# Start of a hybrid-layer kernel: loads queued in order of use, the norm's weight row spread by TensorE, a narrower first projection piece

## The reference

```python
h = jnp.concatenate([meta, x], axis=1)
xn = rms_norm(h, mix_norm_w)                       # the weight row multiplies every token
h = h + hybrid_mixer(xn, w_in, ...)                # proj = xn @ w_in, 3592 columns
h = h + hierarchical_moe(rms_norm(h, ffn_norm_w), ...)   # 32 experts, top 2
out = rms_norm(h, final_norm_w)[:, N_META:]
```

## Time and profile before

| | before |
|---|---|
| median of 3 runs | 1504.84 us (1503.98 to 1507.54) |
| profiled execution | 1506.76 us |
| its span, first to last instruction | 1504.9 us |
| mean granted TensorE clock | 0.935 |
| PE busy | 88% of the span |
| DVE busy | 62% |
| ACT busy | 48% |
| POOL busy | 11% |
| DMA, mean of the span | 182 GB/s |
| chain that ended last, by engine | PE 64%, DVE 13%, ACT 10%, issue 10%, DMA 2% |

### The profile page before, as it was taken

How to read it: one execution, slowest core, us unless ns; L and a number is a source line. 1 busy time by engine, 2 the same in 40 slices (tenths; PEclk the granted TensorE clock), 3 DMA queues, 4 the chain that set the end, 5 groups by cost and what they waited for, 6 DMA issues and landing times.

```text
span 1504.9 us, 20632 instructions
## 1 busy us (share of the span) xinstructions
PE 1318.8 (88%) x7574; PEld 1144.4 (76%) x7574; DVE 932.9 (62%) x1178; ACT 722.3 (48%) x927; POOL 158.7 (11%) x145
## 2 busy tenths in 40 slices
PE   3989998999899989769993389999999999999960
PEld 3979997999799989547772278888888888888840
DVE  4664455445544554332225578888888888888827
ACT  6351234134313430232222067777777777777823
POOL 0010111011102110011110011111111111111000
PEclk9999998999899999659996599999999999999985
DMA  6100010000000000243330379999999999999848
GB/s 194 43 15 29 15 43 16 29 29 29 16 29 29 29 15 26 87 149 103 93 99 23 137 279 356 370 378 383 382 389 372 382 382 379 375 376 377 328 176 334
DMA packets 37141, 274.39 MB, mean 182 GB/s; under 512 B 8053, under 2 KB 8309, under 8 KB 23773
## 3 DMA queue, kind: packets, MB, share of 16 engines
q1 hardware_dynamic: 27032, 250.88, 45.3%
q0 software_dynamic: 9216, 17.06, 3.0%
q10 hardware_dynamic: 837, 5.63, 1.1%
HBM read 260.57 MB, written 29.49 MB: 193 GB/s over the span
## 4 chain that ended last, share of the span: by engine, by line
PE 64%; DVE 13%; ACT 10%; issue 10%; DMA 2%; DVEq 0%; SPq 0%; ACTq 0%; POOLq 0%; POOL 0%
PE bank L1127 7%; PE bank L1129 7%; PE bank L1128 7%; PE bank L511 6%; PE bank L513 6%; PE bank L512 6%; DVE w_lo L744 5%; ACT w_hi L623 4%; PE bank L1245 4%; PE bank L1243 3%; PE bank L435 3%; PE bank L436 3%; PE bank L437 3%; ACT xgT_hi L641 2%; DVE arena L897 1%
## 5 line engine op out<-in xcount | busy, mean ns | idle before, releaser
L744 DVE TENSOR_TENSOR w_lo<-w_raw,w_hi 128x2048 fp32r<-128x2048 f32 x192 | 433.3, 2285 | 68.9 <-ACT w_hi L623 68.9
L623 ACT ACTIVATE w_hi<-w_raw 128x2048 fp32r<-128x2048 f32 x192 | 357.3, 1917 | 17.4 <-PE bank L513 14.3
L1127 PE MATMUL bank<-xn_hi,p_hi 128*128 128x346 f32 (+1 forms) x672 | 229.9, 342 | 0.0
L1129 PE MATMUL bank<-xn_hi,p_lo 128*128 128x346 f32 (+1 forms) x672 | 217.1, 323 | 0.0
L1128 PE MATMUL bank<-xn_lo,p_hi 128*128 128x346 f32 (+1 forms) x672 | 217.0, 323 | 0.0
L511 PE MATMUL bank<-w_hi,xgT_hi 128*128 128x512 f32 x512 | 206.7, 404 | 2.9 <-DVE xgT_lo L890 2.9
L513 PE MATMUL bank<-w_hi,xgT_lo 128*128 128x512 f32 x512 | 201.0, 393 | 0.0
L512 PE MATMUL bank<-w_lo,xgT_hi 128*128 128x512 f32 x512 | 200.7, 392 | 0.0
L1127 PEld LDWEIGHTS bank<-xn_hi,p_hi 128*128 128x128 f32 x672 | 128.6, 191 | 0.4
L1128 PEld LDWEIGHTS bank<-xn_lo,p_hi 128*128 128x128 f32 x672 | 128.2, 191 | 0.3
L1129 PEld LDWEIGHTS bank<-xn_hi,p_lo 128*128 128x128 f32 x672 | 127.6, 190 | 0.0
(11 more groups left out here) (237 smaller groups left out, 2072.9 us busy)
## 6 DMA issues: line engine op xcount, KB each, us to landing
w_raw<-in_w_down SPq DMA_DIRECT2D x32, 2048.0 KB, 9.9
w_raw<-in_w_gate SPq DMA_DIRECT2D x31, 2048.0 KB, 10.6
w_raw<-in_w_up SPq DMA_DIRECT2D x31, 2048.0 KB
p_raw<-in_w_tiles SPq DMA_DIRECT2D x28, 512.0 KB, 3.5
arena<-in_tokens SPq DMA_DIRECT2D x20, 416.0 KB
arena<-y_rows SPq DMA_DIRECT2D x8, 1024.0 KB, 11.9
h_rows<-arena SPq DMA_DIRECT2D x10, 416.0 KB
xn_rows<-arena SPq DMA_DIRECT2D x10, 416.0 KB
```

The lines of the kernel that those rows point to most:

```text
L623: nc.scalar.activation(w_hi[m][:, half], wraw[m][:, half], ACT.Copy).then_inc(hi_done[m], 1)
L744: nc.vector.tensor_tensor(w_lo[m][:, half], wraw[m][:, half], w_hi[m][:, half].bitcast(F32), ALU.subtract).then_inc(lo_done[m], 1)
L1127: nc.tensor.matmul(out[:, 0:n], p_hi[slot][:, k, :], hi, start=(k == 0), stop=False)
L1129: m = nc.tensor.matmul(out[:, 0:n], p_lo[slot][:, k, :], hi, start=False, stop=(k == KD - 1))
```

## The change

SP's list now begins with one row of the norm's weight (4 KB, into row 0 of the last `xn_sb` buffer), then the token tiles with a weight tile behind each of tiles 3, 4 and 5, and at the end the parameters and the other constants, which leave ACT's queue. PE multiplies a column of ones with the row (two float32 matmuls of 512 columns) and DVE copies both results to `mixrow`. The pieces become 312, 364 and 364 tokens: the first is exactly three tiles. PE turns three tiles, then 3 | piece 0 | 4 | piece 1 | 5, 6 | piece 2 | 7 | piece 3 | 8 | piece 4 | 9 | pieces 5 to 8. The lists of ACT and DVE are rewritten to suit; on ACT the high part of `wab_hl` now stands behind the readout of piece 5. Eight semaphores serve the ten token loads.

```diff
-PIECE = [(0, 348), (348, 346), (694, 346)]
+PIECE = [(0, 3 * C), (3 * C, 364), (3 * C + 364, 364)]
+READY = [-(-(o + n) // C) for o, n in PIECE]
...
-            for t in range(4):
+            sp.dma_start(xn_sb[NB - 1][0:1, :], mix_w[0:1, :]).then_inc(s_mix, 16)
+            for t in range(NC):
                 load_x(t)
-            for n, s in enumerate((1, 2, 0)):
-                load_p(s, n)
-            for t in range(4, NC):
-                load_x(t)
+                if t in (3, 4, 5):
+                    load_p((1, 2, 0)[t - 3], t - 3)
+            sp.dma_start(par_sb, par).then_inc(s_const, 16)
+            sp.dma_start(const_sb[:, NFIRST:NCONST], consts[:, NFIRST:NCONST]).then_inc(s_const, 16)
...
-            for t in range(4):
+            pe.wait_ge(s_mix, 16)
+            pe.wait_ge(mix_one, 1)
+            for b in range(2):
+                nc.tensor.matmul(bank[b][0:C, 0:512], r_sb[0:1, 0:C], xn_sb[NB - 1][0:1, b * 512:(b + 1) * 512],
+                                 start=True, stop=True).then_inc(mix_ps, 1)
+            for t in range(3):
                 turn_x(t)
             for n in range(9):
                 pc, s = n // 3, n % 3
-                if n + 4 < NC:
-                    turn_x(n + 4)
-                pe.wait_ge(xlo_done, 2 * (4, 7, 10)[pc])
+                for t in ((3,), (4,), (5, 6), (7,), (8,), (9,))[n] if n < 6 else ():
+                    turn_x(t)
+                pe.wait_ge(xlo_done, 2 * READY[pc])
...
-            act.dma_start(mixrow[0:C, :], mix_w[0:C, :]).then_inc(s_mix, 16)
-            act.dma_start(par_sb, par).then_inc(s_const, 16)
-            act.dma_start(const_sb[:, NFIRST:NCONST], consts[:, NFIRST:NCONST]).then_inc(s_const, 16)
...
+            for t in range(3):
+                token_norm(t)
+            for t in range(NC):
+                xn_high(t)
+                if t == 0:
+                    hi_part(1, 1)
+                if t == 2:
+                    token_norm(3)
+                    hi_part(2, 1)
+                if t >= 2 and t + 2 < NC:
+                    token_norm(t + 2)
+                if t == 3:
+                    hi_part(0, 1)
+                    act.wait_ge(zeros_done, 3)
+                if t >= 4:
+                    first_piece(t - 4)
+            act.wait_ge(s_const, 32)
+            nc.scalar.activation(wab_hl[:, :, 0:8], wab, ACT.Copy).then_inc(wab_done, 1)
+            for n in range(6, 9):
                 first_piece(n)
...
+            for b in range(2):
+                dve.wait_ge(mix_ps, b + 1)
+                nc.vector.tensor_copy(mixrow[0:C, b * 512:(b + 1) * 512], bank[b][0:C, 0:512]).then_inc(mix_done, 1)
...
+            for t in range(3):
+                token_scale(t)
+            for t in range(NC):
+                xn_low(t)
+                if t == 0:
+                    lo_part(1, 1)
+                if t == 2:
+                    token_scale(3)
+                    lo_part(2, 1)
+                if t >= 2 and t + 2 < NC:
+                    token_scale(t + 2)
+                if t == 3:
+                    lo_part(0, 1)
```

More of the change, by code:

```diff
@@ L254, in layer_kernel @@
         s_first, s_const, s_wout, s_ffw = sem("first_loaded"), sem("const_loaded"), sem("w_out_loaded"), sem("ffw_loaded")
-        x_loaded = [sem(f"x_loaded{s}") for s in range(NC)]
+        x_loaded = [sem(f"x_loaded{s}") for s in range(NXS)]
+        mix_one, mix_ps, mix_done = sem("mix_ones_set"), sem("mix_in_psum"), sem("mix_rows_done")
         s_mix, wab_done, abt_done = sem("mix_row_loaded"), sem("wab_done"), sem("abt_done")
@@ L1523, in _ @@
         def _(dve):
+            nc.vector.memset(r_sb[0:1, :], 1.0).then_inc(mix_one, 1)
             for u in range(3):
@@ L1530, in lo_part @@
                                         ALU.subtract).then_inc(p_lo_done[slot], 1)
-            dve.wait_ge(s_mix, 16)
-            for t in range(NC + 1):
-                if t < NC:
-                    dve.wait_ge(rstd_done, t + 1)
-                    if t >= NB:
-                        dve.wait_ge(xt_done, 2 * (t - NB + 1))
-                    nc.vector.scalar_tensor_tensor(xn_sb[t % NB][0:C, :], x_sb[t % NX][0:C, :], nstat[0:C, 2, t:t + 1],
-                                                   mixrow[0:C, :], ALU.mult, ALU.mult).then_inc(xn_done, 1)
-                if t:
-                    for b in range(2):
-                        dve.wait_ge(xhi_done, 2 * (t - 1) + b + 1)
-                        cols = slice((t - 1) * C, t * C)
-                        nc.vector.tensor_tensor(xn_lo[:, 4 * b:4 * b + 4, cols],
-                                                bank[3 + 2 * ((t - 1) % 2) + b][:, 0:4 * C].rearrange("p (k c) -> p k c", k=4),
-                                                xn_hi[:, 4 * b:4 * b + 4, cols].bitcast(F32),
-                                                ALU.subtract).then_inc(xlo_done, 1)
-                if t in (2, 3, 4):
-                    lo_part((1, 2, 0)[t - 2], 1)
@@ new lines, in _, with token_scale @@
+            for b in range(2):
+                dve.wait_ge(mix_ps, b + 1)
+                nc.vector.tensor_copy(mixrow[0:C, b * 512:(b + 1) * 512], bank[b][0:C, 0:512]).then_inc(mix_done, 1)
+            dve.wait_ge(mix_done, 2)
+            def token_scale(t):
+                dve.wait_ge(rstd_done, t + 1)
+                if t >= NB:
+                    dve.wait_ge(xt_done, 2 * (t - NB + 1))
+                nc.vector.scalar_tensor_tensor(xn_sb[t % NB][0:C, :], x_sb[t % NX][0:C, :], nstat[0:C, 2, t:t + 1],
+                                               mixrow[0:C, :], ALU.mult, ALU.mult).then_inc(xn_done, 1)
@@ new lines, in xn_low @@
+            def xn_low(t):
+                cols = slice(t * C, (t + 1) * C)
+                for b in range(2):
+                    dve.wait_ge(xhi_done, 2 * t + b + 1)
+                    nc.vector.tensor_tensor(xn_lo[:, 4 * b:4 * b + 4, cols],
+                                            bank[3 + 2 * (t % 2) + b][:, 0:4 * C].rearrange("p (k c) -> p k c", k=4),
+                                            xn_hi[:, 4 * b:4 * b + 4, cols].bitcast(F32), ALU.subtract).then_inc(xlo_done, 1)
+            for t in range(3):
+                token_scale(t)
```

5 lines of the change are left out of this document (3 added, 2 removed).

## The result

| | before | changed |
|---|---|---|
| median of the runs | 1506.19 us (1503.98 to 1507.7, 4 runs) | 1494.61 us (1493.05 to 1495.56, 4 runs) |
| ratio | | 0.9921 (0.9908 to 0.9933) |
| profiled execution | 1506.76 us | 1494.58 us |
| its span | 1504.9 us | 1492.7 us |
| mean granted TensorE clock | 0.935 | 0.935 |

The change makes the kernel 11.6 us faster by the medians and 12.2 by the two profiled executions. The forecast was 1496.2 us, 8.6 us less than the median of before as it then stood (1504.84 us of three runs; with the fourth it is 1506.19). The measured median lies 1.6 us under the forecast and within its range, but the gain itself is 3.0 us larger than forecast.

What follows compares the result with a forecast made beforehand. The first projection's start, then PE's own work, was taken as the bound: projections start 11.6 us earlier, about 11.5 remain after piece 5, the 2.3 us wait leaves 8.6, so 1504.84 becomes 1496.2 us; range 1492.5 to 1499.8.

Steps and rivals of the forecast that it cites:

- PE's first instruction needs the first constants: Kernel start: constants issued at 0.72 us take 4.8 us to land, so PE begins at 5.5 us.
- The loads are off this path: Start: token tiles, about 2.0 us each, land before ACT asks; cover 5 us for tile 3, 2 to 3 us after.
- no more than 2 us: Start: time allowed for each weight tile loaded between token tiles, giving tiles 4, 5, 6 at about 15.6, 19.6, 23.6 us.
- Rival 3: First transfers late: tile loads over 3.6 us each would set the start; at 4.0 us, 1497.4 us; chance 0.05.
- rival 5: No effect: lists start no earlier because another wait holds PE to 30 us; 1504 us; chance 0.04.
- That part of the change by itself buys little: Start: the weight row spread by PE is ready at 9.9 us, only 0.7 us sooner than the 10.56 before.
- Rival 4: Matmul time rises in steps (1577 us) or has a floor under narrow ones (1506 us); chance 0.03 together.
- Rival 2: Scan and rounds: narrow pieces cover waits less, at worst 1499.4 us, wide ones more, at best 1493.0; chance 0.08.
- The new wait: Ahead of z: PE waits 2.3 us for DVE's convolutions behind `wab_hl`; z starts at 70.9 us, 8.6 us earlier.
- Rival 1: The clock falls in PE's wait ahead of z, costing 1.7 us more: 1497.9 us; chance 0.37.
- nearly even: Odds given to the clock falling in the wait ahead of z: chance 0.37, against 0.43 for the forecast.
- Behind it … sum zero: All 28 weight tiles: 672 matmuls narrower, 1344 wider, at 0.41 ns a column, cancel to no change.

Runs made afterwards that it cites:

- wab_early: Changed kernel with ACT making the high part of `wab_hl` one tile's work earlier, behind tile 8, instead of behind piece 5's readout; 1491.11 us, ratio 0.9895.
- after_again: The changed kernel run once more without an edit, beside the other runs on the same chip; 1495.32 us, ratio 0.9925.
- loads_only: Kernel before with only the new order of the loads; weight row as 104 rows, engine lists and pieces as before; 1501.57 us, ratio 0.9957.
- loads_and_row: Kernel before with the new order of the loads and the weight row spread by PE, old lists and widths; 1498.46 us, ratio 0.995.
- row_only: Kernel before with only the weight row spread by PE, its 104-row load on ACT's queue removed; 1505.14 us, ratio 0.9981.
- start_pieces: Changed kernel with the new widths in the first nine pieces alone and 348, 346, 346 in the heads; 1499.73 us, ratio 0.9955.
- narrow_last: Kernel before with pieces of 364, 364, 312 tokens, so the narrow one comes last; 1505.82 us, ratio 0.9992.
- before_filled: Kernel before with 13 and 11 idle matmuls of 346 columns in the last head's two waits; 1507.76 us, ratio 0.9997.
- no_spread: Changed kernel with the weight row loaded as 104 rows on ACT's queue again, not spread by PE; 1495.97 us, ratio 0.9934.

## Why the prediction was right, and where not

**The start.** The mechanism is right: DVE's multiplication of tile 3, then the last of four turns, sets the first projection. It was put at 21.0 and came at 20.1, so 12.5 us earlier than before instead of 11.6. One term was mis-sized, by 2.4 us, more than the 1 us either way that was allowed for it. "PE's first instruction needs the first constants … **5.5 us**": it began at 3.12, and at 2.7 to 3.4 in the eight profiles with a spread row. The 4.8 us to landing of the earlier trace rows was taken for a price of that transfer. In the kernel before nothing looks earlier: the first to wait for the constants is ACT, behind the first norm's square that starts at 5.25, and in the six profiles without a spread row the landing always stands 0.2 to 0.3 us behind that start. So the 4.8 us was most likely the time until something looked; whether the weight row's load beside it also held it up, no run shows. The two matmuls took 3.74 us (3.8 forecast), so the row was ready at 7.6 instead of 9.9.

**"The loads are off this path"** was wrong, and is why 2.3 us at the row became only 0.9 at the projection. The step compared tile loads with the norms that ask for them, and left out the first weight tile: it stands behind tile 3 in SP's list, and its high part ahead of tile 1's high part in ACT's. It landed at 13.05, and the chain goes through it. Tiles 1 and 2 were waited for too (0.29 and 0.41 us). The tile rate of 2.0 us was right (2.1), and from tile 3 on there was cover, as written. Its "no more than 2 us" for a weight tile doesn't follow from its own rate (512 KB at 213 GB/s is 2.5 us), but tile 3 and the weight tile together landed 3.6 us behind tile 2, so it did no harm. Rival 3, late transfers, didn't come: no tile took near 3.6 us. Nor did rival 5, no effect.

**The row's worth.** "That part of the change by itself buys little": 1.2 us at the first projection on the old lists, 1.9 on the new ones, 2.3 and 1.3 by the medians. It was right in kind, but not for its reason: the row came 3 us sooner than before, not 0.7, and other waits took up most of that.

**Widths and matmul time.** The readouts of pieces 6 to 8 begin 4.00 us apart (52.26, 56.26 and 60.25 on ACT), 0.1665 us for a matmul of 364 columns. Matmuls of 312 columns start 0.143 us apart (22 of them from 25.67 to 28.82); 0.166 and 0.144 were forecast. Rival 4, steps or a floor, is refuted. Rival 2, scan pieces of another width, is refuted as a matter of cover: through heads 0 to 2 the gain stays at 5.5 to 6.7 us.

**The new wait.** 2.12 us against 2.3, ended by the low part of the z weights as forecast; `wab_early` shows its cause by taking it away. z began 9.4 us earlier (8.6 forecast, the difference being the start's).

**Rival 1, the clock.** It happened in the profiled execution, at about its forecast price (1.5 us against `after_again`, where 1.7 was written), and not in the second profile of the same kernel; with three falls in five profiles "nearly even" was fair. The Trainium skill (TensorE: Matmul & The Clock Gate, "HAM oscillation — how this bites in real kernels") has bursts parted by waits for data fall back to the lower clock each time, in an example whose waits are longer than this one. These five traces agree with it three times in five.

**"Behind it … sum zero"** is the step that failed. By matmul lengths it holds: heads 0 to 2 are flat. But the stretches at the lower clock elsewhere differ too: 3.5 us lost between z and 115 us, 6.3 us won behind it, 3.3 of them in the last head, where before's two low stretches are missing. The prediction weighed the clock at one place, the new wait, and took it for unchanged everywhere else. That the total came within 1.6 us is in part luck: the unforeseen gain covers the unforeseen loss and more, so that the gain is 11.6 us and not 8.6, and 1.35 us of the difference are hidden because before's median rose from 1504.84 to 1506.19 with its fourth run.

**What stays open** is why the clock's low stretches moved. Four facts stand. The new widths go with fewer of them in the last head: seven profiles of kernels with 312, 364, 364 in the heads have none there. The old widths don't force them: `loads_only` and `loads_and_row` have none there either, while before, `row_only` and `start_pieces` have both. The lengths of the waits there don't decide it alone (`narrow_last`, with a longer wait and none). And filling them buys nothing in the median (`before_filled`). The median gain of 4.8 and 5.0 us that goes with the widths is measured twice, and the mean clock of the runs rises with it; its cause is only that far traced. More profiles of one kernel, which would tell how often each stretch comes, were not taken.

## What to carry to other kernels

When lists are rewritten by hand, look for each small instruction that moves and for everything queued behind it on its engine *and* on the one that waits for it: here a copy of 0.25 us, moved behind a readout, held DVE's convolutions and then PE, and its better place was worth 3.5 us by the two medians (4.7 by the gains within the groups), more than the spread row. Among loads, check the weights' place as well as the tokens'. And where the clock can fall in a wait, a forecast or a comparison of under half a per cent needs several executions of each kernel: the kernel before alone ran from 1503.09 to 1509.44 us within one group, and its one profile lacked a low stretch that thirteen others had.

## What the runs showed of the hardware

- A wait of 2.12 us ahead of z, of an engine at full rate, was followed by the lower clock in one execution and not in another of the same instruction list (0.57 in 70 to 74 us, and 1.00 in both stretches shown). In five profiles with this wait it fell within z in three.
- PE fell to the lower clock without a wait ahead of it: in `wab_early` it waited for nothing from 20 to 90 us and had 0.57 in 73 to 77 us, behind twenty products of 8 columns in 1.99 us.
- The kernel before took 1503.09 to 1509.44 us within one group of 17 runs; the faster of these runs have a mean clock of 0.937 or 0.938 and the slower 0.935.
- Two float32 products of 1 row by 512 columns, the first of the kernel, took 3.74 us.
- With one queue busy the token tiles of 416 KB landed 2.1 us apart (7.32, 9.45; 2.2 in `after_again`); with the weight row's 104-row load beside them on the other queue 2.7 and 3.1 us apart (`no_spread`: 5.40, 8.14, 11.26), so loading one row 104 times delays each tile beside it by 0.5 to 1.0 us.
